# Last head's attention one block ahead, last retention tile last, one reciprocal for gate and norm, key-value norm behind the third latent, shorter attention

## The reference

```python
rq, rk, rv, rg, cq, ckv, kr = jnp.split(proj, IN_SPLITS, axis=-1)
ret = retention_chunkwise(rope(rq), rope(rk), rv)            # 8 heads of 128
ret_out = jax.nn.silu(rg) * head_groupnorm(ret, ret_out_g)   # gate * per-head norm
c_q, c_kv = rmsnorm(cq, q_norm_g), rmsnorm(ckv, kv_norm_g)   # latents of 512 and 256
q_nope, q_rope = split(c_q @ w_uq)                           # 8 heads, 128 + 64
p = softmax(mask((q_nope . k_nope(c_kv) + q_rope . k_rope) * scale))
mla_out = rmsnorm(p . values(c_kv), mla_out_g)               # the norm is over all 8 heads
h = h + concat(ret_out, mla_out) @ w_o
h = h + square(relu(rmsnorm(h) @ w_up)) @ w_down             # d_ff = 8192
return rmsnorm(h[64:320], final_norm_g)                      # the 256 frames
```

## Time and profile before

| | us |
|---|---|
| median of 3 runs | 1147.01 (1146.83 to 1148.44) |
| the profiled execution | 1147.86 |
| its span | 1145.7 |
| TensorE busy in it | 1124.1 (98%) |
| DVE, ACT, POOL busy | 719.4, 603.8, 79.9 |
| TensorE's share of the chain that ended last | 95% |

### The profile page before, as it was taken

The page is one execution under the profiler, slowest core; times in us unless marked ns, Lnnn a source line. Parts: engine busy times, 40 slices in busy tenths (PEclk is TensorE's granted clock), DMA queues, the critical chain, the costliest instruction groups (busy, mean ns, idle before and its releaser), DMA issues.

```text
span 1145.7 us, 16770 instructions
## 1 busy us (share of the span) xinstructions
PE 1124.1 (98%) x6260; PEld 974.7 (85%) x6260; DVE 719.4 (63%) x964; ACT 603.8 (53%) x905; POOL 79.9 (7%) x82
## 2 busy tenths in 40 slices
PE   7999999999989999999999999999999999999997
PEld 6889999999978888888888888888888888888885
DVE  6976877777786666666664544545666665455453
ACT  8565666566655556555554333334555554344343
POOL 0001120211233330000000000000000000000000
PEclk9999999999989999999999999999999999999999
DMA  9544434444445655555555555555555555555541
GB/s 365 197 149 147 150 145 148 148 147 148 147 151 216 213 177 186 194 186 183 183 183 189 193 199 190 184 184 185 188 190 192 193 188 184 184 186 193 199 157 73
DMA packets 29572, 206.63 MB, mean 180 GB/s; under 512 B 3408, under 2 KB 3664, under 8 KB 5200
## 3 DMA queue, kind: packets, MB, share of 16 engines
q1 hardware_dynamic: 29232, 205.58, 50.2%
q10 hardware_dynamic: 288, 0.31, 0.1%
HBM read 203.79 MB, written 2.10 MB: 180 GB/s over the span
## 4 chain that ended last, share of the span: by engine, by line
PE 95%; DVE 2%; ACT 2%; DMA 1%; issue 0%; SPq 0%; DVEq 0%
PE acc L320 56%; PE ps_qn L320 10%; PE ps_qr L320 9%; PE ps_v L320 8%; PE ps_kn L320 8%; PE ps_x L320 2%; DMA x_in<-x_all 1%; DVE lo L982 1%; DVE x_sq L982 0%; ACT hi L677 0%; PE ps_y L320 0%; ACT x_sq L719 0%; ACT xs L715 0%; DVE mla_o L982 0%; PE ps_y L502 0%
## 5 line engine op out<-in xcount | busy, mean ns | idle before, releaser
L982 DVE TENSOR_TENSOR lo<-raw,hi 128x1024 fp32r<-128x1024 f32 (+1 forms) x379 | 463.6, 1224 | 292.4 <-ACT hi L677 288.2
L320 PE MATMUL acc<-xs,hi 128*128 128x512 f32 (+1 forms) x1952 | 586.1, 363 | 0.0
L677 ACT ACTIVATE hi<-raw 128x1024 fp32r<-128x1024 f32 (+1 forms) x379 | 398.5, 1052 | 299.1 <-PE ps_v L320 106.1
L320 PE MATMUL acc<-xs,lo 128*128 128x256 f32 (+1 forms) x1648 | 454.4, 284 | 9.5 <-DVE xs L999 6.7
L320 PEld LDWEIGHTS acc<-xs,hi 128*128 128x128 f32 x1952 | 344.8, 189 | 51.6
L320 PEld LDWEIGHTS acc<-xs,lo 128*128 128x128 f32 x1648 | 311.3, 189 | 17.1 <-issue 6.7
L677 ACT ACTIVATE half_b<-acc 128x256 f32<-128x256 f32 x100 | 38.6, 386 | 155.1 <-PE acc L320 155.1
L320 PE MATMUL ps_v<-hi,hid 128*128 128x512 f32 x256 | 101.4, 396 | 0.0
L320 PE MATMUL ps_kn<-hi,hid 128*128 128x512 f32 x256 | 100.7, 393 | 0.0
L320 PE MATMUL ps_qr<-hi,hid 128*128 128x512 f32 x256 | 100.3, 396 | 0.0
L320 PE MATMUL ps_qn<-hi,hid 128*128 128x512 f32 x256 | 99.6, 393 | 0.0
(11 more groups left out here) (242 smaller groups left out, 969.2 us busy)
## 6 DMA issues: line engine op xcount, KB each, us to landing
raw<-w_up SPq DMA_DIRECT2D x64, 1024.0 KB, 4.7
raw<-w_down SPq DMA_DIRECT2D x64, 1024.0 KB, 4.7
raw<-w_in SPq DMA_DIRECT2D x42, 1024.0 KB, 4.8
raw<-w_o SPq DMA_DIRECT2D x16, 1024.0 KB, 4.7
h_res<-x_frames SPq DMA_DIRECT2D x1, 2048.0 KB, 7.5
x_in<-x_all SPq DMA_DIRECT2D x3, 544.0 KB, 7.6
consts<-consts_in SPq DMA_DIRECT2D x1, 1217.5 KB, 10.2
raw<-w_in SPq DMA_DIRECT2D x2, 512.0 KB, 9.2
```

Source lines behind the costliest of these rows:

```text
L320: return pe.matmul(o, l, m, start=start, stop=stop)
L677: return act.activation(o, i, ACT.Copy)
L982: return dve.tensor_tensor(o, a, b, op)
```

## The change

- Scores: the rope part of the queries is kept in one buffer `qrs` for each of the two heads, in which the other head's rows hold the low part, so that one product takes the place of two: 5 products a query tile in the place of 6. DVE makes it in four subtractions over 32 partitions where there was one, and ACT in two copies. The key side gets one subtraction and two additions.
- Tails: the last 16 keys of both query tiles are put side by side (`pt_in`, 32 columns), with 32 tokens in the third value tile (`ckv_t`, `VALUE_TILES`): one transpose in the place of two, and one product in the place of two. ACT copies the result in two activations with a scale that zeroes the other half (`K_TAIL`), DVE normalizes in four instructions in the place of two.
- Gate and norm: `gate_inv` and one multiplication go; `ret_norm` forms (1 + exp) * root and takes one reciprocal; POOL multiplies `cen` by the gate's z.
- Start: DVE reads cq2 and makes its chunk halves before the key-value norm's chain, and cq3 behind it; the sums for the queries' norm move into V, in front of its fourth bank, and M waits for two of DVE's copies first.
- Head 7: `mla_scores` in front of q 7, `mla_turn` behind q 7, `mla_values` behind k 7, `mla_total` inside v 7 at step 10; ACT and DVE follow. DVE reads the v 7 block only behind `ret_norm(6)` and the reciprocal of the attention norm, and scales all eight tiles.
- Output projection: three spans, steps 0 to 6, 7 to 14 and 15, so that retention tile 7 comes last in both blocks; `ret_var(7)` in block 1 in front of tile 3; ACT computes `gate_exp(7)` and then `ret_root(7)`, both behind the attention tiles. Block 1 raises `chunk_used` by 2 at its end and not in the middle. DVE's list ends there with `ret_norm(7)`, `ret_rest(7)`.

Core of the diff, in the order tensor, scalar, vector, GpSimd:

```diff
-TOKEN_TILES = ((0, P), (P, P), (2 * P, META))
+VALUE_TILES = ((0, P), (P, P), (2 * P, 2 * META))
...
+                    if n % 8 == 7 and not (late and n == 7):
+                        m.then_inc(sem["chunk_used"], 2 if late else 1)
...
+                        if n == 2:
+                            pe.wait_ge(sem["kv_lo"], 1 + KVL // P)
                         if n == 3:
                             pe.wait_ge(sem["kv_var"], 1)
+                            pe.wait_ge(sem["cq_sum"], QL // P)
+                            for t in range(TILES):
+                                m = mm(cq_col[:, t:t + 1], cq_ss[:, t * P:t * P + P], ones[:, 0:1])
+                            m.then_inc(sem["col_ps"], 1)
...
-                    mm(o, qr[:, 1, r_], krs[:, j, 0, 0:keys], False, False)
-                    mm(o, qr[:, 0, r_], krs[:, j, 1, 0:keys], False, False)
+                    mm(o, qrs[:, j, r_], krs[:, j, 1, 0:keys], False, False)
                     mm(o, qn[:, 0, q], kn[:, j, 0, 0:keys], False, False)
-                    m = mm(o, qr[:, 0, r_], krs[:, j, 0, 0:keys], False, True)
+                    m = mm(o, qrs[:, j, r_], krs[:, j, 0, 0:keys], False, True)
...
-                pe.transpose(ps_v[0:META, 0:P], probs[:, P:P + META], ident)
-                pe.transpose(ps_v[0:META, P:2 * P], probs[:, Q0K + 2 * P:], ident).then_inc(sem["pt_ps"], 1)
+                pe.transpose(ps_v[0:2 * META, 0:P], pt_in[:], ident).then_inc(sem["pt_ps"], 1)
...
-                mm(ps_qn[:, CHUNK:P], v_all[0:META, 1, col], pt_m[0:META, CHUNK:P], False, False)
-                mm(ps_qn[:, 3 * CHUNK:FRAMES], v_all[0:META, 2, col], pt_m[0:META, 3 * CHUNK:], False,
+                late = ps_qn[:, 0:FRAMES].rearrange("p (n t) -> p n t", n=2)[:, :, CHUNK:]
+                mm(late, v_all[0:2 * META, 2, col], pt_m[0:2 * META, :].rearrange("p (n t) -> p n t", n=2), False,
                    True).then_inc(sem["mla_o_ps"], 1)
...
+            pe.wait_ge(sem["fq_v"], 1)
+            def mla_total():
+                pe.wait_ge(sem["mla_ss"], HEADS)
+                mm(ps_kn[:, 0:FRAMES], ones, sum_sq[:]).then_inc(sem["mla_ss_ps"], 1)
+
             for h in range(HEADS):
                 if h % 2 == 0:
                     mla_queries_keys(h // 2)
                 if h:
                     frames(("gate", h - 1))
                     ret_scores(h - 1)
+                early = h == HEADS - 1
+                if early:
+                    mla_scores(h)
                 frames(("q", h))
-                mla_scores(h)
+                if early:
+                    mla_turn(h)
+                else:
+                    mla_scores(h)
                 if h:
                     ret_values(h - 1)
                 narrow(("k", h))
-                mla_turn(h)
+                if early:
+                    mla_values(h)
+                else:
+                    mla_turn(h)
                 if h:
                     ret_var(h - 1)
-                narrow(("v", h))
-                mla_values(h)
...
+                narrow(("v", h), ready=inside({10: mla_total}) if early else None)
+                if not early:
+                    mla_values(h)
 
             frames(LAST, ready=inside({
-                3: lambda: ret_scores(HEADS - 1), 7: mla_total, 13: lambda: ret_values(HEADS - 1)}))
+                3: lambda: ret_scores(HEADS - 1), 13: lambda: ret_values(HEADS - 1)}))
...
             def mixed(k, j):
                 tile = WO_ORDER[k]
-                if tile == 2 and j == 0:
+                if tile == 3 and j == 1:
                     ret_var(HEADS - 1)
...
-            for span in ((0, HEADS - 1), (HEADS - 1, KT)):
+            for span in ((0, HEADS - 1), (HEADS - 1, KT - 1), (KT - 1, KT)):
                 for j in range(2):
-                    wo_block(j, span=span, ready=lambda k, j=j: mixed(k, j))
+                    wo_block(j, span=span, ready=lambda k, j=j: mixed(k, j), late=j == 1)
...
+            def cq_round(k):
...
-            cq_block(0)
-            cq_block(1)
+            for k in range(2):
+                wide_of(("cq", k))
+                cq_round(k)
             act.wait_ge(sem["ss_x_ps"], 1)
...
+            wide_of(("cq", 2))
             act.wait_ge(sem["kv_var"], 1)
             act.activation(kv_f[:], kv_var[:], ACT.Sqrt, bias=eps, scale=1.0 / KVL).then_inc(sem["kv_sd"], 1)
-            cq_block(2)
+            wide_of(("cq", 3))
+            cq_round(2)
             act.wait_ge(sem["kv_scaled"], 2)
             copy(ckvs[:, :, 0:TOK], ckv[:]).then_inc(sem["kv_hi"], 1)
-            cq_block(3)
+            for k in range(KVL // P):
+                copy(two(ckv_t[:, 0, k, :]), tails(ckv[:, k, :])).then_inc(sem["kv_hi"], 1)
+            cq_round(3)
...
+                early = h == HEADS - 1
+                if early:
+                    mla_exp(h)
+                    ret_decay(h)
                 q_block(h)
...
                 crossed(("k", h), zk, swk)
-                mla_turned(h)
+                if not early:
+                    mla_turned(h)
                 if h:
                     ret_root(h - 1)
-                v_block(h)
+                if early:
+                    mla_square(h)
+                    split_hi(CHUNK_OF["v", h] + 2, 0)
+                    act.wait_ge(sem["mla_ss_ps"], 1)
+                    act.activation(rstd[:], ps_kn[:, 0:FRAMES], ACT.Sqrt, bias=eps,
+                                   scale=1.0 / (HEADS * HD)).then_inc(sem["mla_sd"], 1)
+                    split_hi(CHUNK_OF["v", h] + 2, 1)
+                else:
+                    v_block(h)
                 if h:
                     ret_round(h - 1)
-                mla_square(h)
+                if not early:
+                    mla_square(h)
...
+            for k in range(3):
+                mla_round(k)
             split_hi(C_GATE7 + 2, 0)
-            mla_round(0)
+            mla_round(3)
+            mla_round(4)
             ret_out(g)
             b_copy(C_GATE7, HALF_OF[LAST])
-            mla_round(1)
-            mla_round(2)
-            mla_round(3)
-            ret_root(g)
-            gate_exp(g)
-            for k in range(4, HEADS):
+            for k in range(5, HEADS):
                 mla_round(k)
             split_hi(C_GATE7 + 2, 1)
+            gate_exp(g)
+            ret_root(g)
...
+            dve.tensor_scalar(fq_x[:], ps_y[:, 0:2], EPS / D, EPS * EPS, ALU.mult, ALU.add).then_inc(sem["fq_x"], 1)
+            cq_sum(2)
+            split_lo(CHUNK_OF["cq", 2] + 2, 1)
             dve.wait_ge(sem["kv_sd"], 1)
             dve.reciprocal(kv_var[:], kv_f[:]).then_inc(sem["stat"], 1)
             dve.wait_ge(sem["stat"], 2)
...
-            cq_block(2)
+            cq_sum(3)
+            split_lo(CHUNK_OF["cq", 3] + 2, 1)
             dve.wait_ge(sem["kv_hi"], 1)
             tt(ckvs[:, :, TOK:], ckv[:], ckvs[:, :, 0:TOK].bitcast(F32), ALU.subtract).then_inc(sem["kv_lo"], 1)
+            for k in range(KVL // P):
+                dve.wait_ge(sem["kv_hi"], k + 2)
+                tt(two(ckv_t[:, 1, k, :]), tails(ckv[:, k, :]), two(ckv_t[:, 0, k, :]).bitcast(F32),
+                   ALU.subtract).then_inc(sem["kv_lo"], 1)
+            cq_rest(2)
+            cq_rest(3)
 
...
-            cq_block(3)
...
-                tt(qr[:, 1, :], qr_u[:], qr[:, 0, :].bitcast(F32), ALU.subtract).then_inc(sem["qr_lo"], 1)
+                dve.wait_ge(sem["qr_hi"], 2 * p + 2)
+                for j in range(2):
+                    for n in range(2):
+                        own, other = 64 * n + 32 * j, 64 * n + 32 * (1 - j)
+                        tt(qrs[other:other + 32, j, :], qr_u[own:own + 32, :], qrs[own:own + 32, j, :].bitcast(F32),
+                           ALU.subtract).then_inc(sem["qr_lo"], 1)
...
+                dve.wait_ge(sem["gate_exp"], g + 1)
                 dve.wait_ge(sem["ret_sd"], g + 1)
-                dve.reciprocal(r[:], z[:]).then_inc(sem["ret_inv"], 1)
+                dve.scalar_tensor_tensor(out=gate[:], in0=gate[:], scalar=1.0, in1=z[:], op0=ALU.add,
+                                         op1=ALU.mult).then_inc(sem["gate_den"], 1)
+                dve.wait_ge(sem["gate_den"], g + 1)
+                dve.reciprocal(r[:], gate[:]).then_inc(sem["ret_inv"], 1)
                 dve.wait_ge(sem["ret_inv"], g + 1)
-                tt(r[:], cen[:], r[:], ALU.mult).then_inc(sem["ret_y"], 1)
-                dve.wait_ge(sem["ret_y"], g + 1)
                 dve.wait_ge(sem["gate"], g + 1)
-                dve.scalar_tensor_tensor(out=cen[:], in0=r[:], scalar=gain(G_RET + g), in1=gate[:], op0=ALU.mult,
+                dve.scalar_tensor_tensor(out=cen[:], in0=cen[:], scalar=gain(G_RET + g), in1=r[:], op0=ALU.mult,
                                          op1=ALU.mult).then_inc(sem["ret_a"], 1)
...
+                early = h == HEADS - 1
+                if early:
+                    mla_softmax(h)
+                    mla_norm(h)
                 q_sum(h)
```

(71 more changed lines are left out.)

147 lines of the change are left out of this document (57 added, 90 removed).

## The result

The changed kernel took 1140.53 us (median of 6 runs, 1139.68 to 1141.54) against 1147.01 for the kernel before: a ratio of 0.994 with an interval of 0.9928 to 0.9953, 6.5 us faster. The profiled execution is of the first: it took 1139.69 with a span of 1137.8, where that of before took 1147.86 with 1145.7. The kernel before has two groups too: of its six runs here, four took 1146.7 to 1147.0 and two 1148.1 and 1148.4; by its time and its mean granted clock (0.996, not 0.997) the profiled one is of the upper.

The account below looks back on a forecast made before the run. TensorE, busy 1124.1 of 1145.7 us, bounds the kernel. 4.0 (heads 0 to 6) + 2.0 (start) + 2.4 (head 7 to output block 2) = 8.4 us, so 1139.5 profiled, 1138.6 against the median 1147.01; range 1136.3 to 1142.8.

Parts of the forecast that it names:

- the first rival: Wait for `rv` in head 7: the clock falls there, at a price of 2.6 us, giving 1141.2; chance 29%.
- Heads 0 to 6: Score products, a transpose and `mla_values`: fewer TensorE instructions save 0.575 us a head, 4.0 in seven heads (3.2 to 4.8).
- The start: From cq2's read to M: earlier read and fewer waits let M start 2.0 us earlier (bounds 1.2 to 2.2).
- Head 7 to output block 2: From k 7's end to `turn(0)`: old `sq_lo` wait goes, new waits come, 2.4 us gained (1.0 to 3.9).
- its cross-check: Head 7 onward: four waits of 4.85 us replace one costing 6.2, and 0.6 of instructions go; set beside 2.4 gained.
- The rival of the clock: Wait of 2.4 us for `rv`: the granted clock falls in it, costing 2.6 us, 1141.2; chance 29%.
- Moved waits: Head 7 and M: new waits cost what the old did, only counted instructions remain, 1142.4; 14% together with unsaved forms.
- unsaved forms: Heads: 32-row product and strided target cost what the four did, `qrs` quarters come late, 1142.6; 14% together with moved waits.
- late tile 7: Output projection: retention tile 7, now last, comes late and TensorE waits; at 12 us of lateness 1149.8; chance 3%.
- The forecast margin: Step 15 of output block 0: retention tile 7 ready at E + 28.8, step at E + 29.6 (E: k 7's end), 0.8 us spare.
- The slower rival: Retention tile 7 late behind sixteen DVE attention instructions, slowed if run at their rate beside POOL (+ 5.6 us); chance 3%.
- The load of the table: ACT before retention tile 7: 1.28 us a load by the trace; the skill's 2.7, set aside, would give 1140.6.

Follow-up runs that it names:

- the repeat: The changed kernel run once more with nothing altered, against the kernel before: 1141.34 us, ratio 0.9951.
- four scalings on GpSimd: Four of the eight scalings by the attention norm put back on GpSimd, against the changed kernel: 1141.41 us.
- the longer wait: One more reciprocal of 1.75 us, its result unused, ahead of `rv` on DVE, against the changed kernel: 1143.43 us.
- two last steps: Two last steps of output block 1, not one, behind block 0's step 15, against the kernel with early v 7 read and last `gate_z` on DVE: 1138.46 us.

## Why the prediction was right, step by step

The mechanism held: instructions taken off TensorE's list pay in full, the old waits go, and the new waits are the forecast ones. The sizes need two remarks.

The forecast for the profiled execution was 1139.5, and it took 1139.69. That it is so near is in part luck: the three parts were off by -0.5, +0.7 and -0.5 us and nearly cancel (8.4 forecast, 8.10 measured up to `turn(0)`).

Against the median of before the forecast was 1138.6, and that was 1.1 to 1.4 us too low even for the three runs in which the clock held (1139.7 to 1140.0); the median, 1140.53, lies between the two groups, and inside the range because the first rival came on top in three of six runs. The likely reason for the 1.1: the 6.2 us for the old wait, 3.6 and a fall of 2.6, were read from an execution of the upper group of the kernel before. Its two groups lie some 1.3 us apart, close to the 1.1 that a fall of 2.6 costs more than one of 1.5. The median run of before, in the lower group, would then have had less to lose at this place. No trace of such a run is there to show it.

- **Heads 0 to 6**: 4.0 forecast, 3.52 measured. The score products and the transpose were right (0.22 and 0.11 a head). The mis-sized term is `mla_values`: 0.23 taken, 0.17 measured, between my bounds of 0.12 and 0.26; the two 32-row products cost more than half of what the four 16-row ones did. No wait of TensorE in a head shows in the view, and in front of `mla_turn(7)`, where 0.2 was forecast, it is 0.05.
- **The start**: 2.0 forecast, 2.67 measured. The wait for cq2 went as said. kr took 6.01, not the 6.24 of a block behind a wait; DVE was at `kr_t` at 54.32, not 55.1, so no wait was left before M where 0.2 was forecast; 0.18 is the earlier first transfer. The run with the old order lost only 1.3: the wait in front of M stays away in it, so that part of the gain doesn't hang on the order of the reads.
- **Head 7 to output block 2**: 2.4 forecast, 1.91 measured up to `turn(0)` (8.10 less 6.19). The waits: 0.65 / 0.34 for `mla_total`, 2.4 / 2.17 for `rv`, none / none for tile 7, 1.6 / 1.6 for `turn(0)`. From k 7's end the points came at 5.57 (5.55 forecast), 11.73 (11.7), 30.04 (29.6) and 32.34 (31.9); the 0.4 at the end is instructions behind the wait for `rv`: `ret_scores(7)` and the three products of the values took 1.69 where I counted 1.45, and the thirteen steps behind `ret_values(7)` took 4.75 where thirteen at 0.35 are 4.55. `mla_total` took 0.70 where I counted 0.45, but the wait for `rv`, which ends by DVE's time, took that up: it is one reason why it was 2.17 and not 2.4. k 7 ended 0.52 later against its head, not 0.4. Two small errors of the working don't reach the forecast: its cross-check (waits of 4.85 for 6.2, and 0.6 of instructions) gives 1.95 and not 2.4, and the low end of the range takes 3.7 for this part where its bound is 3.9.
- **The rival of the clock** (29%) had the mechanism right and the size wrong: 1.5 us, not 2.6. I had taken its length from the fall behind 3.6 us, which is low for 6.8 us (327.15 to 333.95; the working says near 333.5, but that half microsecond still reads 0.54); behind 2.2 us it is half as long. With the wait at 3.8, the profile has the 6.8 and the 2.6 again. Its chance was also too small: by the group of its time, the fall came in 3 of 6 runs of the result and in 5 of 5 of the repeat.
- **Moved waits, unsaved forms, late tile 7**: excluded by the waits (0.34, 2.17 and 1.6, together 4.1, where those that went cost 1.4, 0.9 and 6.2), by the score rows, and by the 0.7 us of margin. The forecast margin was 0.8; tile 7 and step 15 both came 0.4 to 0.5 later than forecast. That it is thin is seen in the run that read v 7 first: one product held back by 4.3 us cost more than the shorter wait for `rv` had won. The slower rival named this contention, but at a place (the scalings) where the run with four of them on GpSimd shows no cost. In the changed kernel itself the contention was there, unnoticed in the forecast: DVE's eight remainders took 4.23 beside GpSimd's two products, and 3.24 where GpSimd was the one held.
- **The load of the table** took 1.28 both times, as in the earlier trace rows, and ACT's next instruction starts as it ends (323.42 and 1.28, next at 324.71). So the 1140.6 that the working derives from the higher figure has nothing in the trace for it.

## What to carry to other kernels

A thing taken out of the bound engine's list pays in full; a moved one pays only down to the next wait, so write down every new wait with its size before making the move, and count with a fall of the clock behind any wait of some 2 us, at 1.5 us a time here, as a matter of chance. And before giving GpSimd a product in the last chain, look at what VectorE does beside it: if it runs two-input instructions without a pause, put the product on VectorE, or let VectorE wait for it.

## What the runs showed of the hardware

- A 128x256 product on GpSimd takes 0.86 us, or 5.15 and 4.78 when VectorE runs nine or ten instructions with two SBUF inputs back to back beside it; both times it ends 0.6 us behind VectorE's half chunk, the last of that run. The rows don't tell what decides which engine is held: where the product started 0.16 us behind `sq_lo` on VectorE (321.80 and 321.64, the kernel after) it took 0.86, and VectorE's eight instructions 4.23; where it started 0.15 behind (321.16 and 321.01) it took 5.15, and they 3.24. The Trainium skill (SBUF — State Buffer, Who interferes with whom) says that a VectorE instruction with two SBUF inputs contends with a GpSimd instruction that reads SBUF, and that the order of issue decides who blocks. The traces agree with the first; on the second, the product starts behind `sq_lo` and ahead of the eight instructions in both traces, with opposite results, and GpSimd, where it lost, waited not for one instruction but for the whole run of them.
- The granted clock fell to half at the same 2.2 us wait in some executions and not in others: by the groups of their times in 23 of the 36 timed runs that have this wait, and in all six with one of 3.8. It fell in none of the 15 runs of the three last variants that read v 7 first and have the product on DVE, whose waits past the first block are 0.3, 0.6 and 1.2 to 1.9. But a wait of 1.9 is not safe: with one of 0.2 two steps ahead of it the clock fell in 2 of 5 runs, and with another of 1.9 there, by the mean clock, in 5 of 5.
- When it falls varies just as much. In the profiles it came inside the wait (before, 2.2 us after TensorE had run dry), at its end (the changed kernel again) or up to 1.6 us after TensorE had resumed (four scalings on GpSimd). Behind TensorE's last product, where no work follows, the low level came after 1.9 us (the longer wait, 1134.28 to 1136.20) in one profile and after 5.3 us (two last steps, 1129.29 to 1134.59) in another, and between these in the rest. So no length of wait seen here is a threshold.
- A fall lasted 3.4 us and cost 1.5, or lasted 6.8 us and cost 2.3 to 2.7. The long one is seen behind the waits of 3.6 and 3.8 and of twice 1.9, the short one behind those of 2.2 and behind the single 1.9.
